# One decoder layer on one core: state-space scan in groups of four tokens, and the work around the first expert pairs rearranged

## What is computed

```
q | k | v | u = x @ w_in + b_in                  512 columns each
att = LongNet attention, 8 heads of 64, dilated causal windows, ALiBi
ssm = S5: 32 groups of 16 channels, 64 complex states each:
      s_t = Lambda_bar s_(t-1) + B_bar u_t ;  y_t = Re(C s_t) + D u_t ; then gelu and GLU
h = LN1(ALPHA x + [rms(att) | rms(ssm)] @ w_out + b_out)
y = LN2(ALPHA h + PEER(h) + sigmoid(h @ w_ple_gate) * (p @ w_ple))
PEER: per token 8 heads; queries h @ w_pq against 2 x 128 keys; the 16 best of each
      half, the 16 best sums of their pairs; 128 experts a token, each a row of u and v:
      sum over experts of weight * gelu(h . u_e) * v_e
```

## Time and profile before

| | us |
|---|---|
| time, median of 3 runs | 1949.74 (1948.12 to 1951.41) |
| the profiled execution | 1951.28 |
| its span in the profile | 1949.5 |
| PE busy | 1326.9 |
| DVE busy | 1350.4 |
| ACT busy | 793.6 |
| POOL busy | 777.9 |

### The profile page before, as it was taken

How to read it: one execution, slowest core, us unless ns; L and a number is a source line. 1 busy time by engine, 2 the same in 40 slices (tenths; PEclk the granted TensorE clock), 3 DMA queues, 4 the chain that set the end, 5 groups by cost and what they waited for, 6 DMA issues and landing times.

```text
span 1949.5 us, 23865 instructions
## 1 busy us (share of the span) xinstructions
PE 1326.9 (68%) x7204; PEld 646.9 (33%) x7204; DVE 1350.4 (69%) x3212; ACT 793.6 (41%) x2757; POOL 777.9 (40%) x796
## 2 busy tenths in 40 slices
PE   7999886774764866656664655555746666677876
PEld 6765572331232333324321222122221333322221
DVE  6967898864748779888987753444444467886665
ACT  2132247772424344544543443333333223354554
POOL 0953324443434444455443333233233344444442
PEclk9999996776886677777776677766767555576977
DMA  7012689999999999999999999999999999999997
GB/s 299 1 44 93 200 312 421 397 373 421 411 387 415 352 421 421 421 421 420 417 391 416 421 414 420 420 421 421 422 412 422 421 420 405 412 416 417 413 422 287
DMA packets 101024, 723.17 MB, mean 371 GB/s; under 512 B 12016, under 2 KB 12784, under 8 KB 20784
## 3 DMA queue, kind: packets, MB, share of 16 engines
q0 software_dynamic: 82944, 604.02, 75.5%
q1 hardware_dynamic: 17968, 117.77, 15.4%
HBM read 714.78 MB, written 4.87 MB: 369 GB/s over the span
## 4 chain that ended last, share of the span: by engine, by line
DMA 37%; PE 22%; DVE 13%; ACT 7%; issue 6%; POOL 1%; POOLq 0%; ACTq 0%; DVEq 0%; another core or an unknown queue 0%
DMA R<-d_uv,W 37%; PE bank L1408 8%; DVE R L2169 7%; PE bank L1321 3%; PE bank L1295 3%; PE bank L1162 3%; ACT W L1682 1%; ACT L1679 1%; PE bank L1291 1%; PE bank L1154 1%; ACT W L1687 1%; PE bank L1355 1%; POOL R L919 1%; PE bank L1208 1%; ACT W L1650 1%
## 5 line engine op out<-in xcount | busy, mean ns | idle before, releaser
L919 POOL DMA_INDIRECT R<-d_uv,W x576 | 671.8, 1166 | 1011.1 <-PE bank L1408 832.0
L2169 DVE CUSTOM_DVE_ANT_0 R<-R,W 128x1024 f32<-128x1024 f32 x576 | 696.7, 1223 | 473.1 <-DMA R<-d_uv,W 456.1
L1408 PE MATMUL bank<-R,W 128*32 128x512 f32 x2296 | 473.4, 848 | 558.9 <-ACT W L1687 550.5
L1650 ACT CAST W<-W 128x2 uint32<-128x2 f32 x292 | 55.7, 192 | 883.5 <-DVE W L2169 866.8
L1408 PEld LDWEIGHTS bank<-R,W 128*32 128x32 f32 x2296 | 81.6, 125 | 798.5 <-ACT W L1687 724.6
L1687 ACT ACTIVATE W<-W 128x32 f32<-128x32 f32 x576 | 153.5, 313 | 9.7
L1682 ACT ACTIVATE W<-W 128x1 f32<-128x1 f32 x576 | 138.2, 287 | 9.7
L1321 PEld LDWEIGHTS bank<-E 128*128 128x128 f32 x864 | 123.7, 230 | 35.7 <-issue 35.7
L1321 PE MATMUL bank<-E 128*128 128x128 f32 (+1 forms) x864 | 129.7, 317 | 0.5 <-issue 0.5
L963 PE MATMUL bank<-E,W 128*128 128x256 f32 (+1 forms) x384 | 102.9, 427 | 10.1 <-DMA E<-d_xT 7.9
L963 PEld LDWEIGHTS bank<-E,W 128*128 128x128 f32 x384 | 75.4, 200 | 31.5 <-issue 10.1
(11 more groups left out here) (334 smaller groups left out, 1807.9 us busy)
## 6 DMA issues: line engine op xcount, KB each, us to landing
E<-d_kc SPq DMA_DIRECT2D x8, 2560.0 KB
E<-d_w_pq SPq DMA_DIRECT2D x6, 2048.0 KB, 12.7
E<-d_vc SPq DMA_DIRECT2D x8, 1536.0 KB, 26.2
R<-d_uv,W POOLq DMA_INDIRECT x576
E<-d_w_out SPq DMA_DIRECT2D x4, 2048.0 KB, 12.7
E<-d_vc SPq DMA_DIRECT2D x8, 1024.0 KB, 30.5
W<-d_w_in SPq DMA_DIRECT2D x3, 2048.0 KB, 21.1
W<-d_w_pq SPq DMA_DIRECT2D x3, 2048.0 KB, 8.2
```

The source lines that it names most:

```text
L919: pool.indirect_dma_start(ring[r], None, A["uv"], bass.IndirectOffsetOnAxis(ap=stage[:, half, s:s + 1], axis=0),).then_inc(landed[r], 16)
L1408: last = mm(acc(half, TG * column_group(js[s], half), TG), wsel[:, r, :], ring[r][:, D + half * 512:D + half * 512 + 512], start=False, st ...
L1650: return nc.scalar.copy(stage[:, half, PAIR * x:PAIR * x + PAIR], egall[:, 0, at])
L2169: last = nc.vector.tensor_tensor_reduce(ring[r][:, 0:D], ring[r][:, 0:D], hrep[:, js[s], :], 1.0, 0.0, ALU.mult, ALU.add, dots[:, x, s:s + 1])
```

## The change

- The 512 prompt tokens lie in groups of SUB = 4: the host orders each block's tokens by their place in the group (`step_order`) and orders outputs back. One *u piece* makes 128 columns for all 512 tokens: 128 matmuls with 32 columns of weights, one of four column groups for each place in the group. The sample has a u piece of its own (`us`).
- The scan runs over CHUNKS = 128 groups instead of tokens, so four scans (one a quarter) instead of 16, `ssm_in` four times and `ssm_out` four times. What happens inside a group is a small kernel matrix T (`kernel_of`, 48 small matmuls a quarter), applied in `ssm_out`; D u is folded into it, so `skip_term` is gone. New tables: X (18 operations on DVE) is turned by 32 transposes (`turn_b`), C times powers of Lambda in `make_c` (30 operations of 512 elements on DVE). `z_turn` brings the results to channel order (64 small matmuls in all).
- POOL no longer takes part in the scans; the last state and the sample's steps follow scan 3 on it.
- The q pieces of the second half come before block 0's projection; v piece 1 stands between that projection and the turn; the k pieces of the second half come after the first match, from a second load of their weights; v pieces 2 to 4, `glu_block` 1 to 3 with their gates, and the questions of picks 2 and 3 move into the second list, among pairs 0 to 14.
- pbias is loaded in three parts (0.5, 1 and then the whole 2 MiB). The attention of blocks 1 to 3 starts at pair 4 instead of 1, their projections at 38 instead of 35. The turn of block 1 goes from 9 to 7 pairs behind `PROJECT_AT`; `residual_half(2, 1)` stays at 11. Picks 1 to 3 are placed anew.

```diff
+SUB = 4
+CHUNKS = SEQ // SUB
...
+    order = [x for c in range(3) for x in piece("u", c, 0)] + [("turn_b", g) for g in range(8)]
+    order += [("tm", 0), ("ssm_in", 0)] + piece("us", 0, 0) + [("s_in",)] + piece("u", 3, 0)
...
+    order += [("project_first", n) for n in (3, 2, 0, 1)] + [("piece", number("v", 1, 0)), ("rms_inverse", 0), ("residual", 0), ("root", 0)]
+    order += [("normal", 0, 0), ("normal", 0, 1), ("turn", 0), ("turn_out", 0), ("put_v", number("v", 1, 0)), ("ask", 0, 0, 0), ("ask", 0, 0, 1)]
...
-ATT_AT = 1
-GLU_AT = 7
-PROJECT_AT = 35
+ATT_AT = 4
+PROJECT_AT = 38
...
+    for b, glu in ((1, 1), (2, 3), (3, 5)):
+        at[glu].append(("glu_block", b))
...
+    for b, t in ((2, 0), (3, 1), (4, 2)):
+        at[t].append(("piece", number("v", b, 0)))
...
+    look_rest(8, 2)
+    look_rest(14, 3)
...
-    pick(1, 0, 0, 0, 0, 0, 1, 2, 3, 4, 5)
-    pick(2, *range(6, 22, 2), 22, 23)
-    pick(3, *range(24, 40, 2), 40, 41)
+    pick(1, 1, 2, 3, 4, 5, 6, 7, 8, 9, 10)
+    pick(2, *range(17, 27))
+    pick(3, 25, 27, 29, 31, 32, 33, 34, 35, 37, 38)
...
-    project(1, 1, t + 2, t + 5)
-    norm(1, t + 6)
+    project(1, 1, t + 2, t + 4)
+    at[t + 5].append(("root", 1))
+    at[t + 6] += [("normal", 1, 0), ("normal", 1, 1)]
     project(2, 0, t + 4, t + 7)
     project(2, 1, t + 6, t + 11)
-    at[t + 9].append(("turn", 1))
+    at[t + 7].append(("turn", 1))
     norm(2, t + 15)
-    at[t + 11].append(("turn_out", 1))
+    at[t + 9].append(("turn_out", 1))
     project(3, 0, t + 10, t + 14)
-    look(t + 12, 4)
+    look(t + 9, 4)
...
+            load(w_again, eight(A["w_in"][1]), in_w[1])
...
+            load(pbias_second, A["pbias"][:, :, SEQ - 2 * P:SEQ], in_pb)
+            sp.wait_ge(proj_full, len(PIECES))
+            load(parts_of[0][2], eight(A["w_pq"][2]), in_pq[2])
...
+            sp.wait_ge(glu_full, QB)
+            sp.wait_ge(sc_biased, 2 * NH)
+            load(pbias, A["pbias"], in_pb)
+            sp.wait_ge(pq_full, 3)
             load(parts_of[0][3], eight(A["w_pq"][3]), in_pq[3])
...
+                for j in range(4):
+                    for k in range(DC):
+                        for step in range(SUB):
+                            o = bank[32 * step:32 * step + 32, c, j * P:j * P + P].rearrange("p (a b) -> p a b", a=QB)
+                            last = mm(o, w_u(c)[:, k, 32 * j:32 * j + 32], xT_by_step[:, :, k, step, :],
+                                      start=(k == 0), stop=(k == DC - 1), skip_group_check=True)
...
+                for j in range(4):
+                    for x in range(2):
+                        for step in range(SUB):
+                            r = slice(32 * step, 32 * step + 32)
+                            mm(bank[r, 4, j * P:j * P + 32 * (SUB - step)], Bs[:, 4 * q + j, x, :],
+                               C[:, 4 * q + j, x, 0:SUB - step, :].rearrange("p a b -> p (a b)"),
+                               start=(x == 0), stop=False, skip_group_check=True)
...
+                for j in range(4):
+                    mm(bank[:, 5, j * P:j * P + P], T[:, 4 * q + j, :], ut[:, 4 * q + j, :], start=True, stop=False,
+                       skip_group_check=True)
+                    if j == 0:
+                        pe.wait_ge(hs_ready, q + 1)
+                    for x in range(2):
+                        last = mm(bank[:, 5, j * P + 1:j * P + P],
+                                  C[:, 4 * q + j, x, 1:SUB + 1, :].rearrange("p a b -> p (a b)"),
+                                  H[:, x, j, 0:CHUNKS - 1], start=False, stop=(x == 1), skip_group_check=True)
```

More of the change, by code:

```diff
@@ L135, with number, piece_bank @@
+def number(kind, c, x):
+    return PIECES.index((kind, c, x))
+def piece_bank(n):
+    kind, c, x = PIECES[n]
+    if kind in ("k", "q") and x == 0 or kind == "u":
+        return c
+    if kind == "us":
+        return 4
+    if kind == "v" and c < 1:
+        return 3
+    return 6 + n % 2
 UNITS = [(qb, h) for qb in range(QB) for h in range(NH)]
 def order_of_front():
-    steps = 4 * QB
-    pieces = {n: [2 * CT + 2 * n, 2 * CT + 2 * n + 1] for n in range(9)}
-    pieces.update({n: [2 * CT + 9 + n] for n in range(9, 12)})
@@ L144, in order_of_front @@
[L144 to L207, removed]
-    order += [("tops", 0, 1, j) for j in range(4)]
-    order += [("free", 5, 0), ("ask", 0, 2, 0), ("ask", 0, 2, 1), ("free", 1, 2), ("ask_out", 0, 2)]
@@ L210, in order_of_front, with unit, turned, piece @@
-    order += [("ask", 0, 3, 0), ("ask", 0, 3, 1), ("free", 2, 3),
-              ("ask_out", 0, 3), ("match", 0, 2), ("match_out", 0, 2), ("match", 0, 3), ("match_out", 0, 3)]
+    def unit(k, *whats):
+        return [(what, i) for what in whats for i in (2 * k, 2 * k + 1)]
+    def turned(k):
+        return unit(k, "turn_probs", "invert") + [("copy_pt", 2 * k + 1)]
+    def piece(kind, c, x):
+        n = number(kind, c, x)
+        return [("piece", n), ("put_v" if kind == "v" else "put", n)]
@@ new lines, in _ @@
+            sp.wait_ge(hs_ready, CT)
+            load(wout_first[1], eight(A["w_out"][1]), in_out[1])
+            sp.wait_ge(y_full, CT)
+            load(glu, A["glu"], in_glu)
+            load(w_again, eight(A["w_in"][1]), in_w[1])
+            sp.wait_ge(carried, CT)
+            sp.dma_start(A["stp_out"], sm[:, 14:16, :]).then_inc(outs, 16)
+            sp.wait_ge(proj_full, number("q", CT - 1, 1) + 1)
+            load(wout_first[0], eight(A["w_out"][0]), in_out[0])
+            sp.wait_ge(proj_full, number("v", 1, 0))
@@ L725, in _ @@
+            rows(0)
+            sp.wait_ge(at_full, 1)
+            sp.wait_ge(at_squared, 1)
+            load(parts_of[0][0], eight(A["w_pq"][0]), in_pq[0])
             sp.wait_ge(sx_ready, 1)
@@ L932, in piece, with piece_us @@
+            def piece_us():
+                pe.wait_ge(in_xs, 16)
+                pe.wait_ge(bt_put, 8)
+                for c in range(CT):
+                    for k in range(DC):
+                        last = mm(bank[:, 4, c * ST:c * ST + ST], w_u(c)[:, k, :], xS[:, k, :], start=(k == 0),
+                                  stop=(k == DC - 1))
+                last.then_inc(proj_full, 1)
             def piece(n):
                 kind, c, x = PIECES[n]
-                part = "qkvu".index(kind)
@@ new lines, in z_turn @@
+            def z_turn(q):
+                pe.wait_ge(y_used, q + 1)
+                if q == 0:
+                    pe.wait_ge(t_ready, CT)
+                else:
+                    pe.wait_ge(z_ready, q)
+                for step in range(SUB):
+                    for j in range(4):
+                        last = mm(bank[32 * j:32 * j + 32, 4, step * P:step * P + P],
+                                  ident[:, 32 * step:32 * step + 32], zt[:, j, :], start=True, stop=True)
+                last.then_inc(z_turned, 1)
@@ L2383 @@
     r = {n: r["d_" + n] for n in made}
-    y, v = r["y"], r["v_out"]
-    k = r["k_out"].transpose(1, 0, 2).reshape(AW, TOK).T
+    back = np.concatenate([np.argsort(step_order()), np.arange(SEQ, TOK)])
+    y, v = r["y"], r["v_out"][back]
+    k = r["k_out"].transpose(1, 0, 2).reshape(AW, TOK).T[back]
     stp = r["stp_out"].transpose(1, 2, 0).reshape(2, 1, 1, NG, NS)
```

801 lines of the change are left out of this document (479 added, 322 removed).

## The result

The changed kernel takes 1980.72 us (median of 4 runs, 1972.79 to 1983.17) against 1950.58 of the kernel before in the same runs: ratio 1.0148, 95% interval 1.0117 to 1.0179. It is slower by 29 to 30 us; 1954 (1936 to 1971) was forecast, so the time lies outside the range. The profiled execution took 1980.87, with a span of 1979.0.

The account below looks back on a forecast made before the run. TensorE bounds the front, DMA gathers of expert rows the rest. Earlier start -29.4, more bytes +26.6 and idle DMA +7.0 sum to +4.2 us: 1955.5 against the profiled execution, 1954.0 on the median's scale, range 1936 to 1971.

Parts of the forecast that it names:

- The front: Stretch up to the first gather, bound by TensorE: first gather 29.4 us earlier, at about 239 us instead of 268.2.
- 10 of gaps: Before the first gather: new TensorE waits for tables, hand-overs to ScalarE or VectorE and late loads, +10 us.
- over 90% busy: Sign that the forecast is right: TensorE over 90% busy up to the first gather.
- The bytes: Behind the first gather: 697.1 MB instead of 685.9 left to move, 11.2 MB more at 421.5 GB/s, +26.6 us.
- Idle DMA behind the gather, +7: After the first gather: DMA idle 7 us more, from block 1's turn, the first pairs and the attention.
- The turn of block 1, +4.5: At block 1's turn: waiting for block 2's residual drains the eight-slot ring; 9 to 10 us idle, +4.5.
- The first pairs, +2.5: Pairs 0 to 14: added TensorE work delays the ring, moved loads largely fill the gaps; +2.5 us (-3 to +6).
- w_pq's last part: DMA works meanwhile: At pair 14: TensorE waits for this load, queued behind pbias on SP, but DMA stays at work.
- The attention, 0 (0 to +5): Blocks 1 to 3, three pairs later with pick 2 at pairs 17 to 26: no added DMA idleness, 0 to +5 us.
- B: Rival, chance 0.18: TensorE's low clock puts the first gather at 250 and costs the first pairs 14 us; 1972 us.
- A: Rival, chance 0.31: most front hand-overs cost nothing (-35.4) and the ring covers turn and first pairs; 1940.9 us.
- C: Rival, chance 0.14: bytes and start as forecast, but block 1's turn wait is covered; 1949.4 us, no change.

Follow-up runs that it names:

- e7: The changed kernel with four more 2 MiB loads of w_pq's last part, from about pair 53 on: 1994.83 us, ratio 1.0221.
- e2: The changed kernel with the residual of block 2's second half at pair 46 instead of 49: 1972.41 us, ratio 1.0095.
- e1: The changed kernel with question halves of picks 2 and 3 one pair apart and sums of blocks 1 and 2 at pairs 4 and 6: 1972.16 us.
- e8: e5 with the fourth part of w_pq issued ahead of the whole pbias instead of behind it: 1957.91 us, ratio 1.0038.
- e5: The changed kernel with the edits of e1 and e2 together: 1964.03 us, ratio 1.0075 (1.0048 to 1.0102).
- e11: e8 with pick 1's last four operations one pair later and its first cross at pair 4: 1957.45 us, ratio 1.0031 (1.0016 to 1.0047).
- e3: The changed kernel with pick 2 spread over pairs 14 to 27 instead of 17 to 26: 1979.77 us, ratio 1.0141.
- e6: e5 with pick 3 at pairs 31 to 40 instead of 25 to 38: 1964.37 us, ratio 1.0077.
- e9: e8 with pick 2 at pairs 14 to 23 and pick 3 at pairs 31 to 40: 1957.98 us, ratio 1.0037.
- e10: The kernel before with the residual of block 2's second half at pair 43 instead of 46: 1947.55 us against 1950.03, ratio 0.9996.

## Why the prediction was wrong

**The front: right.** The sum was built on TensorE's records. Measured up to the turn (groups by line, columns as in the earlier trace rows):

```profile
L971 PE MATMUL bank<-E,W 128*32 128x128 f32 x1024 | 35.8, 308 | 16.9 <-DMA E<-d_xT 10.5 <-issue 4.3 <-ACT W L1685 2.0
...
L1141 PE MATMUL bank<-E,R 128*128 128x127 f32 x64 | 10.7, 294 | 0.0
...
L1124 PE MATMUL bank<-E,R 128*128 128x128 f32 x64 | 8.1, 279 | 1.4 <-ACT R L1604 1.4
...
L1155 PE MATMUL bank<-W,ident 128*32 128x128 f32 x128 | 4.3, 276 | 0.0
L1033 PE MATMUL bank<-ident,E 128*128 128x128 f32 x32 | 3.9, 280 | 0.0
```

The grouped u pieces were priced 35.8 and took 35.8; the small turns 4.5 and 4.3; the state inputs 7.8 and 8.1; the state outputs 11.4, while their two groups (L1141 and L1136) interleave and stand for some 13 us on the timeline. The kernels inside a group were priced 8: each of the four runs 2.2 us on the timeline. The 32 transposes were priced 7.9 and took 3.9: the row they were priced from is 1.97 us for eight, and in this kernel the same eight take 1.09 (205.82 below). That row was one at the lower clock: the granted clock was 0.55 in 231 to 234 us before and 1.00 in 204 to 210 us after. Up to the end of block 0's projection, before and after:

```profile
0.00:220.60 220.60, 206.72 (x1368) 137.34 (x1370) 172.71 (x368) 59.51 (x162) 96.40 (x200) 0.98 0.32 121
0.00:198.60 198.60, 167.73 (x2245) 142.09 (x2246) 106.46 (x275) 60.34 (x150) 53.70 (x110) 0.94 0.34 129
```

TensorE's busy time fell by 39.0 us (38.3 forecast), but its idle time rose by 17.0, where 10 of gaps and 2.5 of the first load were taken. In the whole front it is idle 33.3 of 240.4 us, so "over 90% busy" failed (86%). Against this, the way from the norm's start to the gather came out 2.3 us shorter (41.7 instead of 44.0), which the prediction did not have. So the sum of the records is right, and that 240.40 lies so near to 239 is in part luck.

```profile
194.97 3.60 PE L1243 MATMUL bank<-R,E 128*128 128x512 f32 x8
198.41 7.03 PE L1012 MATMUL bank<-W,E 128*128 128x512 f32 x16
205.82 1.09 PE L1376 MATMUL bank<-ident,E 128*128 128x128 f32 x8 [0.38 <-DVE E L2349]
```

```profile
198.69 1.28 DVE L2310 SCALAR_TENSOR_TENSOR E<-bank,ssq,E 128x1024 f32<-128x1024 f32 x1 [8.47 <-PE bank L1243]
...
217.97 0.29 DVE L2229 MAX8 E<-W 128x8 f32<-128x128 f32 x1 [11.61 <-ACT W L1801]
```

The projection ends at 198.6 (before 220.6), the turn follows at 205.82 and the first search starts at 217.97 (before 244.90).

**The bytes: right.** 727.52 MB in all, 30.3 ahead of the gather. e7 puts the price of a byte there at 0.7 to 0.9 of the full rate's.

**"Idle DMA behind the gather, +7": the step that failed.** It measured +30.3. The time is outside the range by this term alone: the other two are within 2 us.
- "The turn of block 1, +4.5": right in mechanism, wait (10 us forecast, 12.28 measured) and place, wrong in size: +9.6 between the windows, 8.3 us in the time by e2. The prediction took 9 to 10 us of idle DMA, about TensorE's own wait, less 5.4 before; the windows lost 13.8 and 4.2. TensorE's wait grew by only 1.9 us, but POOL's from 9.90 to 16.24, because no pair's sum stands between projection and turn any more.
- "The first pairs, +2.5": the moved transfers did fill the gaps of pairs 0 to 3, as forecast: DMA moved 396 to 421 GB/s in each ten us from 250 to 290 us, while POOL waited 8.52 and 9.45 us. The sum stopped there. Behind these pairs the transfers are done, and the sums and the question of pick 2 stand as one block of 14 us ahead of pair 8's sum, behind a stretch in which VectorE was full. The windows of 300 to 340 us lose 14.9 us, 13.7 more than before. The work was added up (21.4 + 11.4 + 15 us) but not laid beside the ring's 20 us piece by piece. e1 shows 8.6 us for it.
- "w_pq's last part: DMA works meanwhile": TensorE's wait was 5.7 us and DMA was indeed full then, but the load itself could have been moved in the hole at 320 us. e8 gives 6 us in the medians; its interval overlaps e5's, that of e11 with the same edit does not.
- "The attention, 0 (0 to +5)": +9.7 in the changed kernel, +4.0 in e8. Some 2 us of this window are scatter: e2, whose order is the same up to pair 46, has 355 GB/s in it where the changed kernel has 346. Three placements of picks (e3, e6, e9) changed nothing that can be told, though the last two took 10 and 14 us of VectorE's work out of the window. Whether the rest is the attention's own chain at the lower clock or follows from what the ring holds on entering it stays open; no run separates these.

**The rivals.** B had the time (1972) nearest to the result and named the crowded first pairs with 14 us, but put its start on the front's clock and a gather at 250. The front's granted clock was 0.95 and the gather came at 240.40, so that part did not happen, and its 14 us meet the measured 13.7 by luck; the low clock is only some 3 us of them, as e1's rows show. The clock of 0.50 in 300 to 310 us goes with TensorE's idleness behind a full VectorE. There the sums' 24 records took 5.28 us, 0.22 each; 8 of them took 1.05, 0.13 each, in e1 at full clock. The Trainium skill (TensorE: Matmul & The Clock Gate, HAM oscillation — how this bites in real kernels) tells of a TensorE that waits between bursts of matmuls and begins each next burst at the low clock. The trace agrees at this place (5.54 and 3.90 us idle, clock 0.50), not in the front. A and C asked for covered waits; they were not.

The Trainium skill (DMA: Bandwidth & Descriptors, Where 436 GB/s comes from) has transfers between HBM and SBUF bound at about 358 GB/s. The measurement decides against it for this core, which runs alone: full slices of the changed kernel stand at 420 to 425 GB/s.

With the three cheap edits (e8) the change is still 0.38% slower than before (0.14 to 0.62). No version here is shown to beat the kernel before: e10's interval includes no change. What an earlier start of the DMA-bound stage gives is paid back by the bytes that had lain ahead of it for nothing.

## What to carry to other kernels

Where a stage is bound by DMA, an earlier start counts only with the bytes and the idle time behind it; 27.8 us of start brought nothing here. Write the order of the engine that frees the ring's slots down as stretches between two frees and compare each single one with what the ring holds (here 20 us, less whatever VectorE has just eaten): a sum over the stage hides the one stretch that empties it. Before placing a wait, list what its releaser has in front of it in its own order; here a residual four pairs behind the turn emptied the whole ring. Compare windows only where the granted clock is the same.
